# Five RWKV input chunks as seven block products each, a copy moved ahead of a tangent, and seven expert loads issued in four steps

## The reference, cut to what matters

```
h = rms_norm(x, norm_mix)
proj = h @ w_in                              # 256 x 1024 times 1024 x IN_COLS
u_pool, u_rwkv, u_nsa = split_cols(proj, ...)
  # rwkv7_mixer: u_prev is u one token earlier
  u = u + (u_prev - u) * mu                  # the "shift", per channel
  r, k, v, wd, ad, gd = split_cols(u, [512, 512, 512, 32, 32, 96])
merged = g0 * (y_pool @ wb0) + g1 * (y_rwkv @ wb1) + g2 * (y_nsa @ wb2)
x = x + merged @ w_out
h = rms_norm(x, norm_ffn)
x = x + hier_moe(h, ...)                     # top 2 of 8 experts in the top one of 4 groups
```

## Time and profile before

| | |
|---|---|
| median of three runs | 633.4 us |
| the profiled execution's own time | 633.66 us |
| its span, first to last instruction | 631.9 us |
| PE busy | 591.3 us, 94% of the span |
| DVE busy | 255.9 us, 40% |
| ACT busy | 146.0 us, 23% |
| HBM read | 157.07 MB, 250 GB/s over the span |
| mean granted TensorE clock | 0.984 |

### The profile page before, as it was taken

One profiled execution on the slowest core, in us unless ns is written; L12 is line 12 of the kernel. 1 busy time (PEld: TensorE's weight loads), 2 busy tenths in 40 slices (PEclk: granted clock), 3 DMA queues, 4 the chain that ended last, 5 costly groups with the idle time before them and its releaser, 6 DMA issues.

```text
span 631.9 us, 12324 instructions
## 1 busy us (share of the span) xinstructions
PE 591.3 (94%) x5164; PEld 437.3 (69%) x5164; DVE 255.9 (40%) x680; ACT 146.0 (23%) x367; POOL 19.9 (3%) x23
## 2 busy tenths in 40 slices
PE   8999999999999999999999999999988968969595
PEld 8988888878877777778898999894434525514241
DVE  3152348815434666456777765234111011011022
ACT  3101244033235264354331000001110120110114
POOL 1000000000210013001000000000000000000000
PEclk9999999999999999999999999999999998979799
DMA  8594344751111111102386974999999999999994
GB/s 314 188 352 142 129 138 170 298 190 68 68 68 68 69 67 69 68 3 76 127 333 244 422 266 139 418 422 385 425 419 421 420 415 419 423 420 420 421 398 159
DMA packets 27194, 158.99 MB, mean 252 GB/s; under 512 B 2800, under 2 KB 7040, under 8 KB 9344
## 3 DMA queue, kind: packets, MB, share of 16 engines
q1 hardware_dynamic: 24128, 137.71, 55.8%
q10 hardware_dynamic: 3008, 20.45, 7.8%
HBM read 157.07 MB, written 1.07 MB: 250 GB/s over the span
## 4 chain that ended last, share of the span: by engine, by line
PE 61%; issue 22%; DMA 10%; DVE 3%; ACT 1%; POOL 0%; SPq 0%; POOLq 0%; DVEq 0%; ACTq 0%
PE bank L645 25%; PE bank L1314 7%; DMA ring<-experts 4%; DMA hT<-experts 4%; PE bank L1375 4%; PE bank L1384 3%; PE bank L872 3%; PE bank L1264 3%; PE bank L677 2%; PE bank L981 2%; PE bank L1010 2%; DMA ring<-front 2%; PE bank L1030 1%; PE bank L660 1%; DVE work L1916 1%
## 5 line engine op out<-in xcount | busy, mean ns | idle before, releaser
L645 PE MATMUL bank<-hT,ring 128*128 128x256 f32 (+1 forms) x800 | 177.9, 374 | 0.6 <-DMA ring<-front 0.3
L645 PEld LDWEIGHTS bank<-hT,ring 128*128 128x128 f32 x800 | 143.5, 190 | 26.4 <-issue 8.9
L1916 DVE TENSOR_TENSOR work<-bank,table 128x512 f32<-128x512 f32 (+1 forms) x22 | 11.6, 544 | 97.3 <-PE bank L1264 91.5
L1375 PE MATMUL bank<-ring,work 128*32 128x512 f32 (+1 forms) x176 | 34.0, 620 | 8.3 <-DMA t<-experts 6.6
L645 PE MATMUL bank<-yT,ring 128*128 128x256 f32 (+1 forms) x192 | 35.6, 344 | 0.0
L1517 ACT ACTIVATE work<-bank 128x512 f32<-128x512 f32 (+2 forms) x45 | 23.3, 519 | 49.2 <-PE bank L1375 38.1
L645 PEld LDWEIGHTS bank<-yT,ring 128*128 128x128 f32 x192 | 31.7, 191 | 3.3
L1264 PEld LDWEIGHTS bank<-work,tok 128*128 128x128 f32 x224 | 27.7, 202 | 7.2 <-issue 7.2
L1384 PE MATMUL bank<-work 128*128 128x512 f32 (+1 forms) x68 | 30.1, 582 | 1.4 <-ACT work L1517 0.7
L1264 PE MATMUL bank<-work,tok 128*128 128x128 f32 x224 | 27.9, 286 | 3.5 <-issue 3.5
L1314 PE MATMUL bank<-ring,work 128*32 128x512 f32 x256 | 30.8, 595 | 0.4 <-ACT work L1517 0.4
(11 more groups left out here) (293 smaller groups left out, 867.3 us busy)
## 6 DMA issues: line engine op xcount, KB each, us to landing
ring<-front SPq DMA_DIRECT2D x47, 1024.0 KB, 5.0
ring<-experts SPq DMA_DIRECT2D x42, 1024.0 KB, 25.2
work<-experts SPq DMA_DIRECT2D x9, 1024.0 KB, 27.4
ring<-experts ACTq DMA_DIRECT2D x8, 1024.0 KB, 10.9
table<-experts SPq DMA_DIRECT2D x6, 1024.0 KB, 27.1
yT<-experts SPq DMA_DIRECT2D x6, 1024.0 KB, 26.3
hT<-experts SPq DMA_DIRECT2D x4, 1024.0 KB, 24.7
work<-experts ACTq DMA_DIRECT2D x3, 1024.0 KB, 29.7
```

What stands on the lines that cost most here:

```text
L645: return first(pe.matmul(o, l, r, start=(k == 0), stop=(k == n - 1)))
L1375: last = pe.matmul(o[CAP * e:CAP * (e + 1), 0:w], ghidT[:, f, CAP * e:CAP * (e + 1)], down[e][:, f, lo:lo + w], start=(f == 0), stop=(f == 1))
L1916: return dve.tensor_tensor(o, a, b, op)
```

## The change: what it does

1. `SHIFTED = (2, 3, 4, 5, 6)`: rkv2 to rkv6 go through `seven_products`, with the second bank of chunk c (`rkx`c) in bank 2 + c % 2. ACT's copy of them into `raw` is gone; DVE's `add_blocks` writes `raw` instead. The sums have their own places (`early_sums`).
2. On DVE, `add_rows` and the weight sums of the first of these chunks come ahead of the pooling block. In the loop over chunks, DVE does the weight sums of the next chunk, the blocks of this one, and its shift, in this order.
3. In attention's last unit, ACT copies the turned probabilities before the due tangent.
4. The seven `BY_BRANCH` loads are issued at four points (`gated` at 6, 9, 10 and 12: one, one, three and two loads), in another order of places.

The functions `seven_products`, `add_rows`, `add_weights` and `add_blocks` are the same as before, with the place of the sums as an argument; they only stand earlier in the code. The counts of `gate_sums` that later users wait for are raised to match.

```diff
-BY_BRANCH = (4, 7, 11, 17, 18, 14, 22)
+BY_BRANCH = (11, 7, 18, 14, 22, 4, 17)
+BRANCH_LOADS = ((6, (11,)), (9, (7,)), (10, (18, 14, 22)), (NGATED, (4, 17)))
+SHIFTED = (2, 3, 4, 5, 6)
...
         for c in range(1, 7):
             hand(f"rkv{c}", 4 + c % 2)
+            if c in SHIFTED:
+                hand(f"rkx{c}", 2 + c % 2)
...
             for c in range(1, 7):                                  # PE
-                project(f"rkv{c}", C_K + c - 1)
+                if c in SHIFTED:
+                    seven_products((f"rkv{c}", f"rkx{c}"), C_K + c - 1, hT, early_sums, 0, 4 * (SHIFTED.index(c) + 1), range(NBLOCK))
+                    pe_take()
+                else:
+                    project(f"rkv{c}", C_K + c - 1)
...
-                b0 = full(act, f"rkv{c}")                          # ACT
-                give(copy(raw[:, c % 2, :, 1:S + 1], flat(b0)), "raw_ready", f"rkv{c}")
+                if c not in SHIFTED:
+                    b0 = full(act, f"rkv{c}")
+                    give(copy(raw[:, c % 2, :, 1:S + 1], flat(b0)), "raw_ready", f"rkv{c}")
...
-                gate_tanh(gates_due(s))
+                if n + 1 < len(UNITS):
+                    gate_tanh(gates_due(s))
                 early(step)
                 b0 = full(act, f"pT{g}{u}")
                 give(copy(probT[:, n % 2, :], b0[:, :]), "probT_ready", f"pT{g}{u}")
+                if n + 1 == len(UNITS):
+                    gate_tanh(gates_due(s))
...
-            act.wait_ge(q["gated"], NGATE)
-            early_loads(BY_BRANCH)
+            for gated, slots in BRANCH_LOADS:
+                act.wait_ge(q["gated"], gated)
+                early_loads(slots)
...
+            dve.wait_ge(q["hT_odd_ready"], 2 * 4)                  # DVE, ahead of the pooling block
+            add_rows(hT, early_sums)
+            add_weights(C_K + SHIFTED[0] - 1, early_sums)
             dve.wait_ge(q["u_ready"], 2)
...
             for c in range(1, 7):
-                dve.wait_ge(q["raw_ready"], c + 1)
+                if c in SHIFTED[:-1]:
+                    add_weights(C_K + c, early_sums, f"rkx{c}")
+                if c in SHIFTED:
+                    add_blocks((f"rkv{c}", f"rkx{c}"), raw[:, c % 2, :, 1:S + 1], "dve_chain", early_sum)
+                else:
+                    dve.wait_ge(q["raw_ready"], c + 1 - len([n for n in SHIFTED if n < c]))
                 shift(slice(0, P), c, slice(0, 2), slice(2 * c - 2, 2 * c))
                 dve.sem_inc(q["raw_used"], 1)
```

More of the change, by code:

```diff
@@ L655, in project, with seven_products @@
                 pe_take()
+            def seven_products(names, n_chunk, rows, sums, rows_summed, weights_summed, steps):
+                w = chunk(n_chunk).rearrange("p (k c) -> p k c", k=KD)
+                (a11, a12), (a21, a22) = quarters(w)
+                (b11, b21), (b12, b22) = quarters(rows)
+                r1, r2, r3, r4 = sums[0:4]
+                s1, s2, s4 = sums[4:7]
+                products = ((a11, b11, 0), (a12, b21, 0), (a22, r4, 4), (s1, r1, 1), (a21, r3, 2), (s2, r2, 3), (s4, b22, 4))
+                places = ((0, 0), (0, 1), (0, 2), (0, 3), (1, 1), (1, 2), (1, 0))
+                for y in steps:
+                    n, k = y // (KD // 2), y % (KD // 2)
+                    left, right, summed = products[n]
+                    name, at = names[places[n][0]], places[n][1]
+                    if k == 0 and summed:
+                        pe.wait_ge(q["gate_sums"], summed + (rows_summed if n == 2 else weights_summed))
+                    o = begin(name) if y in (0, 4 * KD // 2) else bank[plan[name][0]]
+                    last = mm(o[:, at * P:(at + 1) * P], left[:, k, :], right[:, k, :], k, KD // 2)
+                    if y in (4 * KD // 2 - 1, NBLOCK - 1):
+                        end(last, name)
             pe.wait_ge(q["zeroed"], 1)
@@ L1064, in _ @@
             pe.wait_ge(q["v_ready"], 2)
[L1066 to L1084, removed]
             def gate_blocks(j, steps):
-                seven_products((f"mg{j}", f"mh{j}"), C_GATE + j, hT, 0, 4 * (j - SEVEN[0] + 1), steps)
+                sums = 4 * (len(SHIFTED) + 1)
+                seven_products((f"mg{j}", f"mh{j}"), C_GATE + j, hT, late_sums, sums, sums + 4 * (j - SEVEN[0] + 1), steps)
                 if NBLOCK - 1 in steps:
@@ L2287, in group_scale @@
                 chain(tt(yh, yh, like(stat[:, 8:16][:, :, None], [P, RH, DH]), ALU.mult), "ynorm_ready")
[L2289 to L2308, removed]
@@ L2310, in add_blocks @@
-            def add_blocks(names, o, done):
-                b0, b1 = [full(dve, name) for name in names]
-                p1, p2, p4, p5 = [b0[:, n * P:(n + 1) * P] for n in range(4)]
-                p3, p7, p6 = [b1[:, n * P:(n + 1) * P] for n in range(3)]
-                c11, c21, right = o[:, 0, 0:P], o[:, 1, 0:P], o[:, :, P:S]
-                chain(dve.tensor_copy(c11, p1))
-                chain(tt(c21, c11, p6, ALU.add), hold=False)
-                chain(tt(c11, c11, p2, ALU.add), done, hold=False)
-                dve.wait_ge(q["dve_chain"], chain.count["dve_chain"])
-                chain(tt(block_sum, c21, p5, ALU.add), hold=False)
-                chain(tt(c21, c21, p7, ALU.add))
-                chain(tt(right, like(block_sum[:, None, :], [P, 2, P]), b1[:, 0:2 * P].rearrange("p (m t) -> p m t", m=2), ALU.add),
-                      done, hold=False)
-                chain(tt(c21, c21, p4, ALU.subtract), done)
-                for name in names:
-                    dve.sem_inc(bank_free[plan[name][0]], 1)
@@ L2365, in _ @@
                 if s + 1 < DURING - BEFORE and SEVEN[0] in gate_begun(s + 1):
[L2366 to L2367 removed]
+                    add_rows(hT, late_sums)
+                    add_weights(C_GATE + SEVEN[0], late_sums)
             attended(NG - 1)
             full(dve, f"mh{NGATE - 1}")
[L2370 to L2371 removed]
+            add_rows(yT[:, 8:16, :], late_sums)
+            add_weights(C_BRANCH, late_sums)
             add_gate(NGATE - 1)
```

58 lines of the change are left out of this document (45 added, 13 removed).

## The result

The changed kernel takes 642.61 us (median of four runs, 641.39 to 643.11) against 633.99 us for the kernel before on the same chip. The ratio is 1.0142, with an interval of 1.0131 to 1.0154. It is slower, by 8.6 us, and 2.5 us above the forecast of 640.1 us, 0.2 us outside its range (636.4 to 642.4 us). The profiled execution took 642.54 us with a span of 640.5 us (631.9 before) and a mean granted clock of 0.972 (0.984 before).

What follows compares the result with a forecast made beforehand. PE bounds the kernel to about 433 us, then the experts' weight loads; 633.66 + 6.4 (wait) + 2.0 (clock) - 1.36 (copy) - 0.3 (loads) = 640.4, predicted median 640.1 us, range 636.4 to 642.4.

Steps and rivals of the forecast that it cites:

- the clock term: PE's clock falls to 0.50 after each of two stalls; slow matmuls after the second cost +2.0 us, ends 0 and 2.8.
- nearer 1.5: Cost in us of a third slow stretch after a PE gap in the kernel before, given without a row.
- The first fall is hidden: Slow clock after the rkv3 stall delays PE's rkv3 to rkv6 one to two us, covered by DVE finishing later.
- The seven products and the stall: PE saves 3.4 us by work alone, but late DVE stalls it 3.7 and 4.6 us; L767 starts 6.4 us later.
- DVE keeps ahead, and the change is faster: Rival: DVE's sums and rounds come early enough that PE never waits in rkv2 to rkv6; 628.3 us, chance 0.07.
- The copy: In attention's last unit, ACT's copy before the tangent removes PE's wait ahead of L1030: -1.36 us, otherwise zero.
- The loads: Issuing seven expert loads in four steps ahead of the first release gains only 0.3 us, ends 0 and -0.4.
- the count of 16 chunks: Between 394 and 433.70 us, 16 expert chunks need 40.0 us in 39.7, so the DMA backlog ends at first release.
- the list of signs: What the new profile should show: stalls, start times, clock, DMA share, and first release 5 to 8 us after 433.70.
- the wait: PE waits for late DVE in rkv3 and ahead of L767, delaying L767 by +6.4 us, bounds 5.5 and 7.5.
- more clock lost: Rival: slow matmuls after both stalls, 2.8 and 1.5 us, not overlapping DVE's rounds; 642.5 us, chance 0.06.
- The clock holds: Rival: the stall ahead of L767 shrinks towards 3.5 us and little slow work follows; 638.1 us, chance 0.17.

Runs made afterwards that it cites:

- after_again: The repeat: the changed kernel run and profiled once more without any edit; 642.26 us, ratio 1.0142.
- e_fill: The changed kernel with ten matmuls of unused result on PE ahead of L767, inside the second stall; 639.35 us, ratio 1.0090.
- e_order: The changed kernel with the weight sums of stream chunk 4 behind the pooling block on DVE instead of ahead; 637.46 us, ratio 1.0059.
- e_fill_half: The changed kernel with five matmuls of unused result ahead of L767, covering about half of the second stall; 641.56 us, ratio 1.0123.
- e_fill_first: The changed kernel with seven matmuls of unused result in the stall inside rkv3 alone; 642.12 us, ratio 1.0135.
- e_banks: The changed kernel with the two rate products moved from banks 2 and 3 to 7 and 6; 633.99 us, ratio 1.0007.
- e_both: The changed kernel with chunk 4's weight sums behind the pooling block and the rate products in banks 7 and 6; 628.97 us, ratio 0.9934.

## Why the prediction was right in kind and wrong in size

**The step that failed is the clock term.** The prediction took +2.0 us with an upper end of 2.8; the profile shows 3.69 us from L767 to L777, and 1.07 + 3.00 us in the repeat. The mechanism held, and its size did not. The ends of the term were read from two slow stretches of the kernel before, 1.88 and 2.83 us, as though two examples were the bounds. The first of them is over-read: 5.45 us is the busy time of a row and 3.57 us a distance from start to start. Row against row it is 5.45 - 3.73 = 1.72 us (the same 32 instructions at 497.04 us). The third, "nearer 1.5", is in the trace of the kernel before, behind 6.62 us of idling:

```profile
591.00:595.00 4.00, 3.60 (x20) 1.03 (x24) 0.00 (x0) 0.05 (x1) 0.00 (x0) 0.55 1.02 422
```

Its first 16 instructions take 3.30 us from 591.40 to 594.70, where the next four take 0.43 us, so it cost 1.58 us. The 2.0 us of the forecast are about the mean of the three. Behind the second stall five profiles have 3.69, 3.00, 2.73, 3.01 and 4.25 us, a mean of 3.34. The upper end of 2.8 us lies below four of the five. With 3.3 us and an upper end near 4.3 the forecast would have been 641.4 us and the range would have held 642.6 us, but that is known only with hindsight. The same stretch in e_fill, with no idle time ahead of it, costs nothing; that shows that it is the fall of the clock and not the instructions. The size follows from how long PE then works at 0.50: an estimate from the granted clock of one-us stretches gives 6.3 us (e_order), 6.8 (after_again, e_fill_half), 8.3 (changed kernel) and 9.4 us (e_fill_first), and the loss is 0.43 to 0.45 of each.

**"The first fall is hidden"** held in the first profile, where L767 started at 80.96 against 81.06 worked out. It did not hold in the repeat (1.07 us late) or in e_fill. There and in the repeat the 24 instructions took 2.55 us more than at full rate, where they took 1.43 us more in the first profile, and about 1.1 us came through. The step had put the delay at "one to two us", again from too few examples: DVE's rounds hid a delay of 1.43 us, and of 2.55 us they let 1.07 through. The stall in rkv3 also came out at 3.33 us, shorter than the 3.55 us from which a fall was inferred; in two of the five profiles with this stall unfilled (e_banks, e_fill_half) the clock did not fall there.

**The seven products and the stall** were right. Pooling block at 42.18 us (said: near 42.7), first shift at 49.38 (near 50), stall of 3.33 us (3.7), L767 at 80.96 after 4.54 us of idling (about 81.1, 4 to 5 us), the delay +6.24 us (+6.4). The wait ahead of L767 ends with DVE's block additions, as said. e_banks and e_order show it by taking each cause away. What the prediction had as a rival, "DVE keeps ahead, and the change is faster", is real, in the form of e_both: 629.0 us where 628.3 was worked out. It did not come about by itself, for the reason given there.

**The copy** brought 1.44 us of 1.36 in the profile and 1.8 us (1.1 to 2.4) alone. **The loads** brought 0.2 us alone, with an interval of 0.8 us gained to 0.3 us lost (said: 0.3 gained), so a term as small as this is neither shown nor refuted; a gain of 12.5 us is refuted. Release to end is 198.1 us against 198.2, and the share below 1 ahead of the release was foreseen by the count of 16 chunks. The first release itself came 8.70 us late, where the list of signs had 5 to 8; the missing part is again the clock.

**What is left.** On the profiled executions the change is +8.88 us where +6.74 was summed. The clock makes 1.69 of the difference of 2.14; the wait -0.16, the copy -0.08, the loads 0.15; 0.26 us of delay come between L777 (9.93 late) and L1012 (10.19 late), nearly all of it at one place inside attention, where PE stands 0.28 us longer ahead of L652 at 236.63 us (0.74 us from the start of the group before it, where L645 at 226.43 us stood 0.46), and why it does stays open; and 0.28 us lies outside the span (2.04 against 1.76 us).

Of the rivals, "more clock lost" (642.5 us) named the time that came out. Its chance of 0.06 was too small, and its picture, slow matmuls after both stalls that do not all hide, is that of the repeat; the first profile reached the same time with the second stall alone. "The clock holds" is what e_fill makes by hand, and it comes to 639.35 us with its matrices 1.3 us late.

Open: why the clock falls and returns when it does, so that the same stall costs 2.7 us once and 4.3 us another time, and whether e_fill_half's one short run kept its clock.

## What to carry to other kernels

- Before a wait is added in front of a block of unrelated work on an engine that takes its list in order, look at what the block needs: DVE's pooling block, long ready, stood behind four sums that waited for a load, and PE's next stage stood behind a bank held by the slowest consumer. Moving one line and two bank numbers made 8.6 us of loss into 4.7 us of gain.
- When a stage gets a second consumer with a longer period than the producer (6.84 against 6.26 us a round), what comes behind the stage should not reuse the last bank of it.
- A stall of PE is priced as its length plus a slow stretch, and the second term is a spread: here 1.6 to 4.3 us behind seven gaps of 3.55 us and more and one of 2.39 us, and 0 to 2.6 us behind the stall of 3.3 us in rkv3. Take its mean and its whole width over every example there is, and let the range reach past the largest when there are only two.

## What the runs showed of the chip that I had not expected

- The fall of the clock is not a fixed answer to a gap. The same 3.33 to 3.36 us of idling in rkv3, behind the same instructions, was followed by 24 instructions in 4.37, 5.49 and 5.49 us (changed kernel, e_fill, after_again) and in 2.94 us (e_banks, e_fill_half). The Trainium skill ("TensorE: Matmul & The Clock Gate", Part 1) says of the start of a kernel that the same kernel shows different counts of slow matmuls from run to run; these rows show the like behind a gap in the middle. The same section puts the penalty of that ramp below 1% of a typical kernel's span. Behind the second stall here it is 3.69 of 640.5 us, 0.6%, which is of that size, and is yet two fifths of the 8.9 us that the change cost.
- A shorter gap is no safe gap: 2.39 us was followed by 3.01 us of loss.
- The clock can fall while PE stands still, so that all of what follows is slow from its first instruction. In the changed kernel PE stops at 76.42 us and resumes at 80.96, and between the two the clock is halved (columns as above):

```profile
78.00:79.00 1.00, 0.00 (x0) 0.00 (x0) 0.75 (x2) 0.00 (x0) 0.00 (x0) 0.99 0.00 0
79.00:80.00 1.00, 0.00 (x0) 0.00 (x0) 0.96 (x4) 0.00 (x0) 0.00 (x0) 0.50 0.00 0
```

- In after_again it fell after PE had resumed, behind the same wait. The same program can thus lose its clock at either point.
